# Retention gate branch between the attention heads, first top-16 lists block by block in the wq stage, decoding in single steps

## The reference

```python
z = xn @ w_in                                   # q latent, kv latent, rope key, rq, rk, rv, rg, ga, gb
o_lat = attention over all earlier keys         # 8 heads, softmax; then @ w_uv
o_ret = retention_chunk(state, rq, rk, rv)
o_a = o_lat_v @ w_oa
o_b = (silu(rg) * head_group_norm(o_ret, ret_norm_g)) @ w_ob
h  += (sigmoid(ga) * o_a + sigmoid(gb) * o_b) @ w_out
# expert mixer
q = rms_norm(h, ffn_norm_g) @ w_q               # 1024 x 2048: 8 heads x 2 halves x 128
q = q * rsqrt(mean(q*q) + EPS)                  # per head and half
s = q . sub_keys                                # 128 scores per head and half
sv, si = top_k(s, 16)                           # 16 lists of 16 of 128: the first lists
top_s, top_pos = top_k(sv0 + sv1, 16)           # 8 lists of 16 of 256: the second lists
eid = si0[...] * 128 + si1[...]                 # decoding: 128 expert numbers a token
act = gelu(expert_u[eid] . x);  h += sum(softmax(top_s) * act * expert_v[eid])
```

## Time and profile before

| | us |
|---|---|
| median of 3 runs | 4565.91 |
| lowest, highest | 4564.35, 4571.74 |
| the profiled execution | 4553.57 |
| its span | 4551.5 |
| busy: PE, DVE, POOL, ACT | 3390.4, 2794.0, 2558.5, 653.9 |
| moved by DMA | 1547.05 MB, mean 340 GB/s |

### The profile page before, as it was taken

The page is one execution under the profiler, slowest core; times in us unless marked ns, Lnnn a source line. Parts: engine busy times, 40 slices in busy tenths (PEclk is TensorE's granted clock), DMA queues, the critical chain, the costliest instruction groups (busy, mean ns, idle before and its releaser), DMA issues.

```text
span 4551.5 us, 43346 instructions
## 1 busy us (share of the span) xinstructions
PE 3390.4 (74%) x13416; PEld 1613.0 (35%) x13416; DVE 2794.0 (61%) x6377; ACT 653.9 (14%) x1978; POOL 2558.5 (56%) x2069
## 2 busy tenths in 40 slices
PE   6877776877777777877787777777787766777873
PEld 3433232423333333423342334333343323555331
DVE  1056568645775567656764587557665674777446
ACT  1112110211121011201121112101120101000110
POOL 0006766666666666666666666766566662445432
PEclk8888998898989988999899999989899887989996
DMA  5659999999989999999999998999899997999983
GB/s 169 199 193 344 402 390 341 334 403 399 374 313 380 399 366 330 371 401 380 347 334 402 396 368 305 389 399 376 317 352 400 370 365 239 306 330 332 359 298 125
DMA packets 606553, 1547.05 MB, mean 340 GB/s; under 512 B 92114, under 2 KB 149083, under 8 KB 606323
## 3 DMA queue, kind: packets, MB, share of 16 engines
q0 software_dynamic: 297216, 1082.26, 63.1%
q1 hardware_dynamic: 275828, 454.63, 27.8%
q10 hardware_dynamic: 33280, 7.39, 0.8%
HBM read 1533.93 MB, written 10.13 MB: 339 GB/s over the span
## 4 chain that ended last, share of the span: by engine, by line
DMA 38%; PE 30%; DVE 15%; POOL 7%; issue 6%; ACT 2%; SPq 2%; ACTq 0%; POOLq 0%; DVEq 0%
DMA rows<-in_peer_v_dram,pe_id 24%; PE PS L982 11%; PE PS L661 10%; POOL rows L601 7%; DMA rows<-in_peer_u_dram,pe_id 3%; DVE rows L1653 3%; DMA wbuf<-in_w_oa_dram 2%; DMA wbuf<-in_w_in_dram 2%; PE PS L646 2%; DMA wbuf<-in_w_ob_dram 2%; DMA wbuf<-in_peer_w_q_dram 2%; PE PS L771 1%; PE PS L752 1%; PE PS L899 1%; DVE xr L1678 1%
## 5 line engine op out<-in xcount | busy, mean ns | idle before, releaser
L601 POOL DMA_INDIRECT rows<-in_peer_u_dram,pe_id x1024 | 1277.2, 1247 | 1143.3 <-DVE dots L1653 546.0
L982 PE MATMUL PS<-rows,diags 128*128 128x512 f32 x2356 | 1321.6, 693 | 662.8 <-DMA rows<-in_peer_v_dram,pe_id 497.2
L601 POOL DMA_INDIRECT rows<-in_peer_v_dram,pe_id x1024 | 1262.0, 1232 | 778.2 <-PE PS L982 502.4
L1653 DVE CUSTOM_DVE_ANT_0 rows<-rows,px 128x1024 f32<-128x1024 f32 x1024 | 1245.9, 1223 | 728.3 <-DMA rows<-in_peer_u_dram,pe_id 726.0
L661 PE MATMUL PS<-wbuf,xt 128*128 128x512 f32 (+1 forms) x2304 | 1054.5, 600 | 62.7 <-DMA wbuf<-in_w_in_dram 44.6
L982 PEld LDWEIGHTS PS<-rows,diags 128*128 128x128 f32 x2356 | 460.0, 212 | 1336.9 <-issue 993.5
L661 PEld LDWEIGHTS PS<-wbuf,xt 128*128 128x128 f32 x2304 | 449.2, 201 | 667.2 <-issue 510.9
L1678 DVE SCALAR_TENSOR_TENSOR xr<-rows,gcoef,xr 128x1024 f32<-128x1024 f32 x435 | 558.2, 1283 | 164.1 <-issue 161.1
L661 PE MATMUL PS<-wbuf,wide 128*128 128x512 f32 (+1 forms) x828 | 384.9, 603 | 61.6 <-ACT wide L1047 15.2
L661 PEld LDWEIGHTS PS<-wbuf,wide 128*128 128x128 f32 x828 | 158.8, 198 | 273.3 <-issue 170.2
L1771 ACT ACTIVATE diags<-ident,gcoef 128x128 f32<-128x128 f32 x589 | 209.1, 398 | 154.8 <-DVE gcoef L1669 83.6
(11 more groups left out here) (300 smaller groups left out, 2422.2 us busy)
## 6 DMA issues: line engine op xcount, KB each, us to landing
wbuf<-in_w_in_dram SPq DMA_DIRECT2D x396, 512.0 KB, 11.0
wbuf<-in_peer_w_q_dram SPq DMA_DIRECT2D x144, 512.0 KB, 10.4
wbuf<-in_w_ob_dram SPq DMA_DIRECT2D x72, 512.0 KB, 10.8
wbuf<-in_w_out_dram SPq DMA_DIRECT2D x72, 512.0 KB, 9.5
KV<-in_cache_ckv_dram SPq DMA_DIRECT2D x160, 128.0 KB
wbuf<-in_w_oa_dram SPq DMA_DIRECT2D x36, 512.0 KB, 15.0
rows<-in_peer_u_dram,pe_id POOLq DMA_INDIRECT x1028, 5.6
rows<-in_peer_v_dram,pe_id POOLq DMA_INDIRECT x1024
```

What stands on the lines that cost most here:

```text
L601: pool.indirect_dma_start(row_slot(kind, n), None, a["peer_u" if kind == "u" else "peer_v"][0], bass.IndirectOffsetOnAxis(ap=pe_id[t % 2][ ...
L982: last = nc.tensor.matmul(bank[3 + 4 * c], diag(n), row_slot("v", n)[:, c * 512:(c + 1) * 512], start=start, stop=stop)
L1653: V.tensor_tensor_reduce(out=row, in0=row, in1=px[:, :], scale=1.0, scalar=0.0, op0=ALU.mult, op1=ALU.add, accum_out=dots[:, at_:at_ + 1]) ...
```

## The change

Nothing that is computed changes apart from the place of one scaling. Three things move.

1. **Branch.** The turns of rg and ob no longer follow the heads but alternate with them: head 0, rg, head 1, rg, ... head 4, ob (with bT before it), ... head 7, ob. Both are generators now (`pe_branch`, `act_branch`), and rg lands in `z` instead of `WK`. DVE gates after the score of head 4. The samples keep the old order.
2. **First lists.** Each wq block is followed at once: in the first turn of block i PE turns the queries of block i-1, in the second it scores them (4 lists, one bank), and ACT copies both out, the scores unscaled into `wide`. DVE runs its passes on 4 lists at a time (`choose`), part 0 (max, index) and part 1 (replace, max, index) in different turns. The norm's factor is positive, so the order within a list does not depend on it; it is now applied to the 16 values found.
3. **Decoding.** The comparison, the product and the reduction each get a turn of their own.

```diff
@@ pe_front
                 groups = prob_groups(t)
+                branch = pe_branch(pe, J, t, tj)
                 scores(0)
                 for h in range(NH):
...
                     yield "head"
+                    yield next(branch)
...
             for i in range(4):
-                yield from pe_block(pe, J, t, "wq", i, xt)
-            J.wait_drained(pe, tj, "wq", 3)
-            for i in range(4):
-                transposes(J, tj, pe, "pqT", i, [z[:, (4 * i + k) * P:(4 * i + k + 1) * P] for k in range(4)])
...
+                for half, at_ in enumerate(pe_block(pe, J, t, "wq", i, xt)):
+                    if i > 0:
+                        (turned_queries, key_scores)[half](i - 1)
+                    yield at_
+            turned_queries(3)
+            yield "pqT"
+            key_scores(3)
@@ act_front
+            def turned(i):
+                act_drain(act, J, tj, "pqT", i, lambda b: nc.scalar.activation(WK[:, 4 * i * P:4 * (i + 1) * P], b, ACT.Copy))
+
+            def scored(i):
+                act_drain(act, DD, tj, "pscore", i, lambda b: nc.scalar.activation(
+                    wide.rearrange("p (c g k) -> p c g k", c=2, g=PH)[:, :, 2 * i:2 * i + 2],
+                    b[:, 0:4 * P].rearrange("p (c g k) -> p c g k", c=2, g=2), ACT.Copy))
+
             for i in range(4):
+                if i > 0:
+                    turned(i - 1)
                 yield "wq"
...
                 nc.scalar.activation(z[:, i * BW:(i + 1) * BW], b[:, 0:BW], ACT.Copy).then_inc(J.drained, 1)
+                if i > 0:
+                    scored(i - 1)
                 yield "wq"
@@ dve_front
+                    if h == 4:
+                        gated()
                     yield "head"
+                    if h < NH - 1:
+                        yield "rg" if h < 4 else "ob"
...
+            def choose(i, part):
+                groups = [c * PH + 2 * i + k for c in range(2) for k in range(2)]
+                if part == 0:
+                    DD.wait_drained(dve, tj, "pscore", i)
+                for f in ("max", "index") if part == 0 else ("replace", "second", "second index"):
+                    top_step(link, f, wide, P, sv, si, groups)
+                    link.join(dve)
+
+            for i in range(4):
                 yield "wq"
+            for i in range(2):
+                for part in range(2):
+                    choose(i, part)
+                    yield "wq"
             J.wait_drained(dve, tj, "wq", 3)
...
+            choose(2, 0)
+            yield "pqT"
+            choose(2, 1)
+            yield "top"
+            if not sample:
+                dve_x_norm(dve, t + 1)
+            yield "top"
+            choose(3, 0)
+            yield "xT"
+            choose(3, 1)
             link(dve, V.tensor_scalar(ssq[:, :], ssq[:, :], 1.0 / PD, EPS, ALU.mult, ALU.add))
             r = rsqrt(dve, link, ssq[:, :], 2 * PH, nr)
...
+                half = sv[:, i * PH * TOPK:(i + 1) * PH * TOPK].rearrange("p (h k) -> p h k", h=PH)
+                link.mark(V.tensor_tensor(half, half, spread(r[:, i:2 * PH:2], PH, TOPK), ALU.mult))
+            link.join(dve)
+            yield "linA"
...
                 link(dve, V.tensor_tensor(oh.rearrange("p (s a) -> p s a", s=P), spread(tf[:, :], P, TOPK),
                                           over(edges[:, :], P, TOPK), op))
+                yield "linA"
                 link(dve, V.tensor_tensor(oh4, oh4, table.unsqueeze(2).broadcast_to([P, PH, TOPK, TOPK]), ALU.mult))
+                yield "linA"
                 link(dve, V.tensor_reduce(dst[:, :], oh.rearrange("p (s a) -> p s a", s=P), AX, ALU.add))
-                yield "linA"
```

More of the change, by code:

```diff
@@ L677, in pe_linA, with pe_branch @@
                 yield from pe_block(pe, J, t, "linA", i, xt)
+        def pe_branch(pe, J, t, tj):
+            for i in range(2):
+                yield from pe_block(pe, J, t, "rg", i, xt)
+            ret_gated.wait(pe, t)
+            for i in range(2):
+                transposes(J, tj, pe, "bT", i, [oret[:, (4 * i + k) * P:(4 * i + k + 1) * P] for k in range(4)])
+            J.wait_drained(pe, tj, "bT", 1)
+            for i in range(2):
+                yield from pe_block(pe, J, t, "ob", i, t2)
         def pe_front(pe, t, sample=False):
@@ L1502, in dve_front @@
             yield "linA"
-            for _ in top16(dve, link, cand, PH, NCAND, ts_, tp):
+            for step in ("max", "index", "replace", "second", "second index"):
+                top_step(link, step, cand, NCAND, ts_, tp, range(PH))
+                link.join(dve)
                 yield "linA"
```

169 lines of the change are left out of this document (84 added, 85 removed).

## The result

The changed kernel takes **4421.4 us**, median of 4 runs (4418.5 to 4422.8), against 4565.1 us for the kernel before (4 runs): ratio 0.9681, 95% interval 0.9663 to 0.970. It is faster by 144 us. The forecast was 4440 with a range of 4385 to 4535. The other 13 us of the difference of the medians lie in the profiled execution of the kernel before, which took 12 us less than its median, while that of the changed kernel is at its median.

A forecast was written before the change was run, and what follows sets the result against it. DMA transfers bound the fronts, 42 us each unfed. Per front 6.5 + 7.5 + 3.5 - 2.5 = 15, seven times 105, plus 12 and 9: 126 us off 4553.6, plus 12.3 for the median, gives 4440; range 4385 to 4535.

The forecast's parts named there:

- A: Branch between the heads: idle DMA time in turns 7 to 22 regained, 6.5 us a front, bounds 3 and 9.5.
- The signs named for A: Turns 7 to 22 of the fronts at 390 GB/s or more, near 102 us in the last front.
- B: First lists taken out of turns 47 to 50, DVE's backlog included: 7.5 us a front gained, bounds 4 and 10.
- the backlog: DVE work carried into the first linA turns, claimed to go with the first lists' delay; 7.5 us for both.
- C: Decoding cut up, behind the second group: 3.5 us a front gained, bounds 0 and 8.
- D: The wq stage itself: longer half turns at the lower clock level lose 2.5 us a front, bounds 0 and 6.
- E: The ends: 12 us gained at tile 0's front and 9 in the samples, bounds 10 and 28 together.
- the clock: Rival, wq stage: PE waits for ACT every turn and its granted clock falls, 4604 us at 0.70; chance 0.08.
- Only-part-regained: Rival, fronts: idle time partly moves elsewhere, 4.5 us a front gained plus 21 at the ends, 4514 us; chance 0.20.
- The ceiling on the mean: Rival, fronts: bursts of 401 GB/s need slower stretches between, so only the ends gain, 4545 us; chance 0.05.

The follow-up runs named there:

- the repeat: The changed kernel itself, run again on the second chip: 4408.2 us, ratio 0.9655 to the kernel before.
- the last version: Changed kernel plus finish split, ACT's tanh earlier, turn 0 in two pieces and retention's chain spread: 4419.5 us on the third chip, ratio 0.9517 to the kernel before.

## Why the prediction was right, and where it was off

The reading that carried it held: the fronts are bound by the transfers, the gain is the time in which they are not fed, and 42 us a front were there to be had. 15 a front were forecast and 16.1 came, with 17.5 instead of 21 at the ends: 130.5 us between the profiled executions where 126 were forecast. The forecast of the median is 19 us too high, and 14 of these are the 12.3 us that the prediction added because the profiled execution before lay under its median; after the change it does not. The terms erred in opposite directions, though, and that the sum came out so well is in part luck.

- **A was too large in the changed kernel.** 6.5 forecast; it shows 3.1 in turns 7 to 22 (4.2 with the turns up to 38), while the part alone stays open between 2.6 and 5.9. The step that failed is that "the step that finishes an older tile on DVE" falls in here too and has "a ring in flight to cover" it. The ring of 8 rows covered some 5 us of DVE; the finish is 6.3 to 7.2, and PE waits behind it. With the finish split, turns 7 to 22 get 1.7 us shorter in the mean, half of the 3.4 that are missing. Where the rest went stays open. The signs named for A were missed accordingly: 385 GB/s instead of 390, and 107.9 us in the last front instead of 102.
- **B was about right, but not as it was added up.** 7.5 forecast for turns 47 to 57, 6.1 measured; 28.8 us in tile 5's front against "28 or less". With the lists alone turns 47 to 50 lose 7 us in the mean and turns 51 to 57 nothing: the backlog that I let go with it did not. In the changed kernel turns 47 to 50 lose only 4.2, since the rescaling shares turn 51 with the last list, a piece of 6.0 us, where a turn of its own saves 3 more; turns 51 to 57 lose 2.0, which they do not without the decoding's steps (52.3 us, before 51.7).
- **C was too small.** 3.5 forecast, 6.4 measured in turns 58 to 63, and 8.6 to 10 in all fronts when it alone is undone (across chips). The mechanism was right and its size was off. 9.2 us of idle were read behind the second group, and 3.5 taken, because a piece of 6.5 and the lat turn stay. Both do stay and both still cost: POOL stands 3.9 us behind the first and 4.4 behind the second. But the two pieces of 7.8 and 8.8 had made it stand 3.0 and 5.4, so 4.5 us of waiting went, a us more than the whole term. The remaining 2 of the 6.4 are not traced. The sign held: the slowest 10 us ahead of `chosen` (2650.2 us in tile 5's front) run at 308 GB/s where the earlier trace rows had 167, and the dip behind the lat turn stays, 261 where the earlier trace rows had 242:

```profile
2637.30:2647.30 10.00, 7.86 (x29) 4.18 (x27) 9.93 (x13) 1.72 (x6) 8.07 (x6) 1.00 0.89 308
...
2667.30:2677.30 10.00, 10.00 (x27) 5.20 (x26) 6.14 (x12) 3.07 (x7) 3.83 (x3) 0.87 0.73 261
```

- **D was too large.** 2.5 forecast, 0.6 measured (1.0 in the repeat). Tile 5's front did lose 2.5 (63.0 us at 388 GB/s, granted clock 0.93), the other six between -1.5 and 1.8. Why most fronts hide the longer half turns and this one does not was not traced.
- **E** gave 10.9 at tile 0 and 6.6 in the samples, 12 and 9 forecast. Tile 1's first u row was named at 331 and came at 332.1. Which of the samples' terms fell short was not tried.

The rivals: the clock stayed at 0.92 over the fronts and was 0.93 in the wq stage of tile 5's front, where it had been 0.95. Only-part-regained had A right (3) and B and C too small (4 and 0). The ceiling on the mean is refuted: the fronts average 381 GB/s, and in the last version 389 over 3227 us. The rule of the Trainium skill's DMA: Bandwidth & Descriptors, section Where 436 GB/s comes from, of about 358 GB/s a core from HBM, is not what these traces show: the fronts of the changed kernel average 381 GB/s over 3290 us.

## What to carry to other kernels

Where gathers run through a ring that several engines empty, find the longest unbroken piece on each of them between two rows, and compare it with what the ring rides over. Here, with 8 slots, a piece of 5.3 us was nearly free, one of 6.4 made the issuing engine wait 3 to 4 us, and two slots fewer cost 34 us a front. Cut the longest pieces first; pieces of 2.3 to 3.5 us brought at most 1 us a front over one of 5.3. A piece includes the waits inside it, so a short chain of three engines in one turn can be the largest of all. After each cut look at what the other engine of the ring holds, since taking away one wait (here ACT's tanh) is worth nothing while the piece beside it is as long.
